# A two-layer streaming encoder on eight cores: score blocks whole, recurrence keys ahead, tap loads on another queue, squares later, last stage in half-size blocks

## The reference, cut to what matters

```python
for i in range(2):                                   # x: 2048 positions x 1024 channels a core
    h = rmsnorm(x, g_mix[i])
    q, f, v, og, glu, ga, gb = split(h @ w_in[i])    # 4 x 512, 1024, 2 x 1024 columns
    # mixer A: per head (4 of 128), S_t = diag(f_t) S_{t-1} + k_t v_t^T ; o_t = S_t^T q_t
    o = rmsnorm(recurrence(silu(q), 1 - f, v, log f)) * silu(og)
    # mixer B: 31 taps over positions, 512 channels
    u = silu(layernorm(causal_dwconv(glu_a * sigmoid(glu_b), conv_w[i])))
    x = x + (sigmoid(ga) * (o @ w_br_a[i]) + sigmoid(gb) * (u @ w_br_b[i])) @ w_out[i]
    up = causal_dwconv(rmsnorm(x, g_ffn[i]) @ w_up[i], 3 taps)
    x = x + (silu(up[..., :2816]) * up[..., 2816:]) @ w_down[i]
    x = x + sigmoid(rmsnorm(x, g_ple[i]) @ w_ple_gate[i]) * (p[i] @ w_ple_proj[i])
return rmsnorm(x, g_final)
```

## Time and profile before

| | |
|---|---|
| median of 3 runs | 2245.28 us (2244.7 to 2246.98) |
| the profiled execution | 2240.89 us |
| its span, slowest core (core 1) | 2239.3 us (all cores 2225.9 to 2239.3) |
| TensorE busy | 2083.4 us |
| VectorE busy | 1403.8 us |
| ScalarE busy | 1077.4 us |
| GpSimd busy | 177.1 us |
| granted TensorE clock, mean over the cores | 0.972 to 0.977 |

### The profile page before, as it was taken

How to read it: one execution, slowest core, us unless ns; L and a number is a source line. 1 busy time by engine, 2 the same in 40 slices (tenths; PEclk the granted TensorE clock), 3 DMA queues, 4 the chain that set the end, 5 groups by cost and what they waited for, 6 DMA issues and landing times.

```text
span 2239.3 us, 29208 instructions; the slowest of 8 cores (2225.9 to 2239.3 us)
## 1 busy us (share of the span) xinstructions
PE 2083.4 (93%) x10176; PEld 983.0 (44%) x10176; DVE 1403.8 (63%) x1861; ACT 1077.4 (48%) x1305; POOL 177.1 (8%) x190
## 2 busy tenths in 40 slices
PE   6988999889999999999898899989999999999985
PEld 1454444544444444444344644445444444444432
DVE  4686357554698349965667645575359852996257
ACT  3645155542677147722455532645247732874143
POOL 2120000000001000010000000000000010001000
PEclk8999999999999999999999999999999999999997
DMA  9946445365544665486446464356354366437434
GB/s 150 169 115 121 63 70 85 114 112 87 76 66 54 88 89 80 53 129 130 67 65 111 109 120 76 44 131 139 55 85 76 51 88 107 76 51 106 61 61 156
DMA packets 220854, 206.35 MB, mean 92 GB/s; under 512 B 19867, under 2 KB 195611, under 8 KB 220710
## 3 DMA queue, kind: packets, MB, share of 16 engines
q0 software_dynamic: 175520, 140.89, 44.2%
q1 hardware_dynamic: 45190, 63.59, 9.2%
HBM read 319.07 MB, written 26.26 MB: 154 GB/s over the span
## 4 chain that ended last, share of the span: by engine, by line
PE 78%; DVE 7%; ACT 7%; issue 4%; DMA 3%; SPq 1%; DVEq 0%; ACTq 0%; POOL 0%; POOLq 0%
PE ps L310 78%; ACT arena L319 5%; DVE arena L323 3%; DVE x_sb L323 1%; ACT L319 1%; DVE arena L327 1%; DMA ws_sb<-w_in 1%; DMA x_sb<-xT 1%; DMA arena<-scr_n 1%; DMA scr_u<-arena 0%; DMA arena<-scr_dg 0%; DVE arena L697 0%; DVE S L323 0%; SPq L774 0%; PE ps L861 0%
## 5 line engine op out<-in xcount | busy, mean ns | idle before, releaser
L310 PE MATMUL ps<-h_sb,ws_sb 128*128 128x512 bf16 x5376 | 1209.7, 383 | 33.4 <-ACT arena L319 16.3
L310 PEld LDWEIGHTS ps<-h_sb,ws_sb 128*128 128x128 bf16 x5376 | 526.3, 99 | 680.1 <-issue 71.4
L310 PE MATMUL ps<-arena,ws_sb 128*128 128x512 bf16 x2816 | 641.7, 383 | 21.5 <-ACT arena L319 10.3
L319 ACT ACTIVATE arena<-ps 128x1024 bf16<-128x1024 f32 (+3 forms) x484 | 400.7, 844 | 375.4 <-PE ps L310 358.4
L327 DVE SCALAR_TENSOR_TENSOR arena<-arena,cv_sb 128x1024 f32<-128x1024 bf16 x352 | 432.1, 1279 | 42.3 <-ACT arena L319 40.8
L310 PEld LDWEIGHTS ps<-arena,ws_sb 128*128 128x128 bf16 x2816 | 276.8, 99 | 362.9 <-issue 40.1
L319 ACT ACTIVATE arena<-x_sb 128x1024 bf16<-128x1024 f32 (+1 forms) x120 | 114.7, 969 | 474.1 <-DVE x_sb L323 364.6
L319 ACT ACTIVATE arena<-ps,cv_sb 128x1024 f32<-128x1024 f32 (+2 forms) x272 | 263.6, 971 | 121.2 <-PE ps L310 93.9
L323 DVE TENSOR_TENSOR arena<-arena 128x1024 bf16<-128x1024 f32 (+3 forms) x252 | 247.3, 1002 | 11.9 <-ACT arena L319 6.6
L319 ACT ACTIVATE arena<-arena 128x512 f32<-128x512 f32 (+3 forms) x256 | 203.2, 811 | 31.6 <-DVE arena L327 13.8
L327 DVE SCALAR_TENSOR_TENSOR arena<-arena,ps 128x1024 f32<-128x1024 f32 x64 | 77.8, 1221 | 188.1 <-PE ps L310 167.5
(11 more groups left out here) (56 smaller groups left out, 698.7 us busy)
## 6 DMA issues: line engine op xcount, KB each, us to landing
ws_sb<-w_up POOLq DMA_DIRECT2D x40, 1024.0 KB, 11.1
ws_sb<-w_in POOLq DMA_DIRECT2D x37, 1024.0 KB, 13.0
ws_sb<-w_down POOLq DMA_DIRECT2D x32, 704.0 KB, 8.5
arena<-scr_dg SPq DMA_DIRECT2D x48, 288.0 KB, 3.1
scr_dg<-arena SPq DMA_DIRECT2D x32, 288.0 KB, 3.5
x_sb<-xT SPq DMA_DIRECT2D x32, 256.0 KB, 8.2
ws_sb<-w_out POOLq DMA_DIRECT2D x8, 1024.0 KB, 11.7
ws_sb<-w_ple_gate POOLq DMA_DIRECT2D x8, 1024.0 KB, 11.6
```

The source lines that it names most:

```text
L310: P.op("pe", lambda e: e.matmul(out_ap, l_ap, r_ap, start=start, stop=stop), reads=[l_t, r_t], writes=[out_t], inc=inc)
L319: P.op("act", lambda e: e.activation(out=out_ap, in_=in_ap, func=func, **kw), reads=[in_t] + list(rd), writes=[out_t])
```

## The change

Eight things are changed together.

1. Scores: for each head one 128x128x128 matmul in place of two of 64 columns. The masks are as before.
2. The tiles for the decays (`elc`, `emc`, `mm_`) are kept track of by half (`t_`), in the same memory.
3. In all mixers but the first, the keys of chunk 0 are taken in `closing`, after the forget gate's matmuls, with another order of banks. The recurrence then starts one fill step later and ends one earlier.
4. `scale` takes its second root from bank 3 (the outputs') instead of bank 0 (the transposes'), both logarithms ahead of both exponentials.
5. `get_dg` loads the taps on Pool's queue.
6. The first branch blocks and the layer norm's steps are emitted in another order.
7. `Acc` has lag 3 in mixer and feed-forward, and in `ple` lag 2 with the square issued one block later. Where the half that is scaled next is at hand, the root is read from the tile and not through DRAM. `scale_steps` takes six steps instead of seven; the tap builds come after it. `ple` evaluates block 0 before `flush`, with tanh in half 0.
8. The last embedding pass is `ple_last`: 16 blocks of 512 positions from single banks, its first tile's root taken after half of them, the last table loaded ahead, and the outputs interleaved.

`rec_steps` is moved up in the file unchanged but for what is shown.

```diff
@@ -250,9 +250,9 @@
...
-        elc = Tl(hsm_sb[:, 0, :], "elc")
-        emc = Tl(hsm_sb[:, 1, :], "emc")
-        mm_ = Tl(hsm_sb[:, 2, :], "m")
+        elc_ = [Tl(hsm_sb[:, 0, :], "elc%d" % i) for i in range(2)]
+        emc_ = [Tl(hsm_sb[:, 1, :], "emc%d" % i) for i in range(2)]
+        mm2_ = [Tl(hsm_sb[:, 2, :], "m%d" % i) for i in range(2)]
...
@@ -531,36 +531,43 @@
...
         class Acc:
-            def __init__(self, hf, keep=False, base=NSCR, lag=1):
-                self.hf, self.keep, self.base, self.lag = hf, keep, base, lag
+            def __init__(self, hf, base=NSCR, rsb=NSCR + 4096, lag=3, late=False, direct=False):
+                self.hf, self.rsb, self.lag, self.late, self.direct = hf, rsb, lag, late, direct
...
             def step(self, oc):
                 if oc >= self.lag:
                     self.sums()
-                self.square(oc)
+                if not self.late:
+                    self.square(oc)
+                elif oc > 0:
+                    self.square(oc - 1)
+                    if oc == 7:
+                        self.square(7)

...
-                rs = AR(self.base + 2048 * (self.lag + 1), 4096, F32, "ars")
+                rs = AR(self.rsb, 4096, F32, "ars")
...
-                if not self.keep:
+                if not self.direct:
...
@@ -570,12 +577,12 @@
...
-        def scale_steps(l, hf, gcol, dst):
-            rs2 = load_rs(hf)
+        def scale_steps(l, hf, gcol, dst, acc=None):
+            rs2 = load_rs(hf) if acc is None else acc[0].rs
             yield
             n = 0
-            for i in range(7):
-                for _ in range(3 if i < 2 else 2):
+            for i in range(6):
+                for _ in range(3 if i < 4 else 2):
...
@@ -616,11 +623,12 @@
...
             for g in range(NG):
+                if g % 2 == 0:
+                    next(side, None)
                 d = ring_[g % 4]
                 build_taps(l, g, d, "dve")
                 P.dma("sp", lambda e, d=d, g=g: e.dma_start(out=dg_t[l][g].ap, in_=d.ap), out_t=dg_t[l][g], in_t=d)
                 if g % 2 == 1:
-                    next(side, None)
                     yield
...
@@ -692,6 +698,7 @@
             def gate_ph2(hd, t_):
...
+                elc, emc, mm_ = elc_[t_], emc_[t_], mm2_[t_]
...
@@ -714,12 +721,96 @@
...
+            p_tr, p_sc, p_kv, p_o, p_ss = bank1[0:5]
...
+            def rec_steps():
...
+                def keys(c):
+                    kt = Ktok[c % 2]
+                    for hd in range(4):
+                        hs = slice(hd * 128, (hd + 1) * 128)
+                        P.op("pe", lambda e, hs=hs: e.transpose(p_trb[:, hs], KT[c].ap[:, hs], ident.ap),
+                             reads=[KT[c], ident], writes=[p_tr], inc=(hd == 3))
+                    act(kt, kt.ap, p_tr, p_trb[:, 0:512], AF.Copy)
+                    for hd in range(4):
+                        hs = slice(hd * 128, (hd + 1) * 128)
+                        mm(p_sc, p_sc.ap[:, hs], KT[c], KT[c].ap[:, hs], QT[c], QT[c].ap[:, hs], True, True, hd == 3)
...
+                def outer(c):
...
+                    tt(b_, h3(b_.ap), b_, h3(b_.ap), elc_[c // 4], elc3[:, :, c:c + 1].to_broadcast([128, 4, 128]), ALU.mult)
+                    if c < 7:
+                        tt(b_, h3(b_.ap), b_, h3(b_.ap), emc_[(c + 1) // 4], emc3[:, :, c + 1:c + 2].to_broadcast([128, 4, 128]), ALU.mult)
...
+                def scale(c):
+                    for p_, q_ in ((p_ss, osq_[0]), (p_o, osq_[1])):
+                        mm(p_, p_.ap, ones, ones.ap, q_, q_.ap, True, True, True)
+                    for p_, o_ in ((p_ss, osd[0]), (p_o, osd[1])):
+                        act(o_, o_.ap, p_, p_.ap, AF.Ln, bias=EPS, scale=1.0 / 128)
+                    for o_ in osd:
+                        act(o_, o_.ap, o_, o_.ap, AF.Exp, scale=-0.5)
...
+                keys(0)
+                yield
...
+            rec = rec_steps()
+
             def closing(u0, u1, names):
                 pt = {}
+                if not early:
+                    set_banks((2, 3, 4, 5, 6, 7, 0, 1), ())
                 for nm in ("f", "q", "v", "og"):
                     for u in (u0, u1):
                         pt[u, nm] = gate_mm(u[0], u[1], nm) if nm in names else None
                     wrel(W[nm])
+                    if nm == "f" and not early:
+                        next(rec)
                 for u in (u0, u1):
                     gate_ev(u[0], u[1], *[pt[u, nm] for nm in ("f", "q", "v", "og")])
                 both(u0, u1)
@@ -766,7 +857,7 @@
                     build_taps(l, g, d, "pool" if g % 2 == 0 else "dve")
                     P.dma("sp", lambda e: e.dma_start(out=dg_t[l][g].ap, in_=d.ap), out_t=dg_t[l][g], in_t=d)
                 else:
-                    P.dma("sp", lambda e: e.dma_start(out=d.ap, in_=dg_t[l][g].ap), out_t=d, in_t=dg_t[l][g])
+                    P.dma("pool", lambda e: e.dma_start(out=d.ap, in_=dg_t[l][g].ap), out_t=d, in_t=dg_t[l][g])
...
@@ -848,93 +939,12 @@
...
-            def rec_steps():
...
-                    for hd in range(4):
-                        b0 = hd * 128
-                        mm(p_sc, p_sc.ap[:, b0 + 64:b0 + 128], KT[c], KT[c].ap[:, b0:b0 + 128], QT[c], QT[c].ap[:, b0 + 64:b0 + 128],
-                           True, True, False)
-                        mm(p_sc, p_sc.ap[0:64, b0:b0 + 64], KT[c], KT[c].ap[:, b0:b0 + 64], QT[c], QT[c].ap[:, b0:b0 + 64],
-                           True, True, hd == 3)
...
-                def scale(c):
-                    for i in range(2):
-                        p_, o_ = (p_ss, p_tr)[i], osd[i]
-                        mm(p_, p_.ap, ones, ones.ap, osq_[i], osq_[i].ap, True, True, True)
-                        act(o_, o_.ap, p_, p_.ap, AF.Ln, bias=EPS, scale=1.0 / 128)
-                        act(o_, o_.ap, o_, o_.ap, AF.Exp, scale=-0.5)
...
-            rec = rec_steps()
-            n_side = 29
+            n_side = 29 if early else 28
             n_main = 28
-            lead = 4
+            lead, tail = (4, 0) if early else (5, 1)
             done = 0
             for i, _ in enumerate(fill_steps()):
-                while done * (n_main - lead) < (i + 1 - lead) * n_side:
+                while done < n_side and done * (n_main - lead - tail) < (i + 1 - lead) * n_side:
                     next(rec, None)
                     done += 1
...
@@ -1012,16 +1022,19 @@
...
             y = [None] * 8
-            for cc in range(4):
-                ln_dve(cc)
+            ln_dve(0)
+            ln_dve(1)
+            branch_a(0, 0)
             ln_act(0)
+            ln_dve(2)
+            ln_dve(3)
             ln_act(1)
-            branch_a(0, 0)
+            branch_a(0, 1)
             ln_act(2)
             ln_act(3)
             to_channels()
-            for oi in range(1, 4):
-                branch_a(0, oi)
+            branch_a(0, 2)
+            branch_a(0, 3)
             for oi in range(4):
                 branch_b(0, oi)
...
-            acc = Acc(hf, base=57344 if l == 0 and hf == 0 else NSCR)
+            acc = Acc(hf, 57344, 61440) if l == 0 and hf == 0 else Acc(hf)
...
-            acc = Acc(hf)
+            acc = Acc(hf, direct=hf == 1)
             pend.append(acc.finish)
+            faccs[hf] = acc
...
@@ -1198,53 +1212,132 @@
...
-            first = pg_mm(0)
-            flush()
...
-            acc = Acc(hf, l == n_layers - 1 and hf == 1, 32768, 2)
-            pend.append(acc.finish)
-            accs.append(acc)
-            for oc in range(8):
+
+            def gated(oc, pg, pp):
                 sg, tp = sg2[oc % 2], tp2[oc % 2]
-                pg, pp = first if oc == 0 else pg_mm(oc)
+                if oc == 0 and hf == 0:
+                    act(sg, sg.ap, pg, pg.ap, AF.Tanh, scale=0.5)
+                    stt(tp, tp.ap, sg, sg.ap, 1.0, pp, pp.ap, ALU.add, ALU.mult)
+                    stt(xs[oc][hf], xs[oc][hf].ap, tp, tp.ap, 0.5, xs[oc][hf], xs[oc][hf].ap, ALU.mult, ALU.add)
+                    return
                 act(sg, sg.ap, pg, pg.ap, AF.Sigmoid)
                 tt(tp, tp.ap, sg, sg.ap, pp, pp.ap, ALU.mult)
                 tt(xs[oc][hf], xs[oc][hf].ap, tp, tp.ap, xs[oc][hf], xs[oc][hf].ap, ALU.add)
+
+            gated(0, *pg_mm(0))
+            flush()
+            acc = Acc(hf, *((32768, 38912) if hf == 0 else (67584, 73728)), lag=2, late=True, direct=hf == 0)
+            pend.append(acc.finish)
+            paccs[hf] = acc
+            for oc in range(8):
+                if oc > 0:
+                    gated(oc, *pg_mm(oc))
                 acc.step(oc)
                 if oc % 4 == 3:
...
+        def ple_last(l, W, h, pbt, pbv):
+            set_banks(range(6), ())
+            wgs = [wtile(W["pg%d" % i]) for i in range(2)]
+            wps = [wtile(W["pp%d" % i]) for i in range(2)]
...
+            ost = [AR(53248 + i * 2048, 2048, F32, "ost%d" % i) for i in range(8)]
+            out_tiles.extend(ost)
```

(78 more changed lines are left out.)

145 lines of the change are left out of this document (62 added, 83 removed).

## The result

The changed kernel takes **2181.92 us** in the median of four runs (2180.59 to 2183.37), the kernel before 2246.13 (2244.70 to 2247.01): ratio 0.9714, 95% interval 0.9699 to 0.9729. It is faster by 64 us, where I forecast 110; the time lies 16 us above the top of my range.

A forecast was written before the change was run, and what follows sets the result against it. The tensor engine, busy 2083.4 of 2239.3 us, was taken as the bound, with waits and slow clock to remove. 14.2 + 15.0 + 6.2 + 13.8 + 54 + 6.5 = 109.7 us gave a median of 2136 us, range 2118 to 2166.

The forecast's parts named there:

- the normalization's end: Mixers' branch stage: new order starts ScalarE's work about 1.8 us earlier, lost again waiting for ucs; priced at nothing.
- Sums' lag: Output and down projections: sums three blocks behind end waits of about 1.85 us, seven times, plus 1.3 in first mixer; 14.2 us.
- Embedding stages: Per-layer embedding passes: shorter edge waits and less slow clock, 15.0 us in layer 0; layer 1 6.2 and 13.8.
- the output-gate weights: Start of the mixer after layer 0's embedding: weights' load awaited; 1.5 us charged for wait and clock (0 to 4.5).
- The last stage: Final embedding half to the kernel's end: 57.1 us instead of 70.9, a gain of 13.8 us.
- The later mixers up to the ucs wait: Three later mixers: interleaved stretch of 71.3 us falls to 52.9, 18.4 less; booked as 18 each, 54 us.
- scores: Mixers: four whole score blocks instead of eight halves save 0.90 us a chunk, 32 chunks, 28.8 us.
- the keys: Later mixers: first keys done in the last gates remove a 2.58 us wait before the first outer product.
- the taps: Later mixers' filter pairs: loading taps on Pool's queue costs 0 to 0.2 us for each of six pairs.
- (a): Rival, mixers: VectorE and ScalarE hold them, removed tensor work turns into waits, half of 60 us lost; 2166 us, chance 0.13.
- (b): Rival, mixers: tap loads from Pool's queue land late, 7.1 us, costing 28 us; 2164 us, chance 0.08.
- (c): Rival, mixers: whole score blocks are worth nothing, 28.8 us less gain; 2165 us, chance 0.05.

The follow-up runs named there:

- the base: The changed kernel with the gate weights gb1 and the branch weights (2 MB) held until ucs has landed; 2150.56 us, ratio 0.9587, in the narrowest of three runs.

## Why the prediction was wrong

**The step that failed** is "ucs is awaited from a DMA chain, the idle time of 4 us ... gathers in one place and the clock may fall", with the verdict that the normalization's end "gives a little ... and takes it back". I priced that at nothing. It gave 3.0 to 3.3 us a mixer ahead of the first branch_b, more than my 1.8, and cost 12.1, 11.9, 12.3 and 10.0 behind it, 46.3 us, where the whole forecast is 45.4 off. I had treated the gather's time as fixed (7.6 us from first issue to last landing in the kernel before) and only asked when it would start; it took 14.2. But the edit moves the end of branch_a(0,3) forward against the gather, and with it the release of ga0's slot: 1 MB that had stood 2.9 us behind the gather now stands in front. I did not count the loads that a moved step releases on Pool's queue. That transfers stretch beside one another was there to be read: 1 MB of w_in took 15.0 us next to the stores, 11.3 in the earlier trace rows.

That the loads cause it is shown, not argued: holding 1 MB halves the step, holding 2 MB leaves 1.0 to 5.1 of it, the order alone brings it into the kernel before wherever the loads meet the gather, and over 160 gathers the length goes with the distance of w_br_a. The DMA: Bandwidth & Descriptors page of the Trainium skill (Queues, rings and completion order) says that each DMA engine takes turns packet by packet between the queues that have work for it; the 4.6 and 11.5 us of a transfer of the same gather, without and with the weights ahead of it, are in line with that, though no run here shows the turns themselves or why it is a factor of 2.5. The two loads act at different places: the branch weights lie beside the gather, gb1 beside the stores, whose last must land before the gather may start. Of the 9.8 us that a wait grew in the mean (0.5 to 10.3), 6.6 are the longer gather and 3.5 the lesser work behind its issue (7.5 to 4.0); of these, 1.1 come back when gb1 is held, and the rest, some 2.4, is the price of the new order by itself. That is the part which my "takes it back" had right: in the base the branch stage gives 8.9 us ahead of the first branch_b, all mixers together, and loses 10.0 behind it.

**Sums' lag** (14.2): 13.0 in the changed kernel, 13.5 by the ratios with the edit undone. Right in the seven later stages, 2.0 us each for my 1.85. In the first mixer, where I had 1.3, it lost 1.0: its sums still wait 2.34 us for ScalarE (1.81 before).

**Embedding stages** (15.0 and 20.0): 17.4 and 18.1. The edge waits are 1.42 us where I had 1.2, and the output-gate weights come late as I feared:

```profile
1112.26 3.61 PE L310 MATMUL ps<-h_sb,ws_sb 128*128 128x512 bf16 x16 [1.42 <-DVE arena L323]
...
1121.21 2.95 PE L310 MATMUL ps<-h_sb,ws_sb 128*128 128x512 bf16 x8 [3.62 <-DMA ws_sb<-w_in]
```

The last stage takes 58.1 us from 2123.72 to the end (57.1 forecast); two sums in it wait for ScalarE's square, 2.05 and 2.52 (the root's table loads stand ahead of it in the code), which I had not seen.

**The later mixers up to the ucs wait** (54): 52.6, near enough, but not by my terms. Up to the branch stage they gave 13.8, 16.0 and 13.5, 43.3 us, where I had 18.4 each; the other 9.2 came from the branch order's first half, which I had booked as taken back. Inside, scores were over-sized (28.8; 13 alone, 18 in the base), the keys were worth 7 to 9, and the taps, which I charged, were worth 11 to 14. The pieces were measured by taking each out alone and don't add up to the whole; still, my errors had opposite signs, and the good sum is luck in good part. The common fault: I priced an edit against the stage as it was, while the others changed what it stood beside. How much of the taps' wait comes from the stage being shorter was not run by itself.

**Rivals.** (a), engines other than TensorE taking over in the mixers, is what ate 9 to 10 us of the scores: right in kind, a third of its size. (b), late taps: the median is 4.4 us, but only 36 of the 48 landed in 3.1 to 5.4; the first four of each later mixer, issued behind bulk loads (at 383.8 us in the second), took 10.6 to 14.6. TensorE waited 0.8 us at most all the same. The hold of Pool's queue by VectorE's casts, which the SBUF — State Buffer page of the Trainium skill (the "DVE blocks DMA" trap) would have allowed, was not tested, and no wait shows one. (c): halves cost TensorE more than wholes in the changed kernel too, eight in 1.19 us at 386.12 with halves against four in 0.39 at 387.23 in the base. The cycles that I took from the Trainium skill's page TensorE: Matmul & The Clock Gate (Back-to-back issue gap) stand there for isolated matmuls, and the page itself says that they count too little at few columns, where each matmul has its own weight load; they were no price for these halves. But a part of (c)'s price came by way of (a). No rival named a DMA that grows longer because another is issued sooner, and that one decided.

## What to carry to other kernels

When an edit moves work forward, list every load whose buffer the moved step frees, and set its issue against each small latency-bound transfer near it: some three to five microseconds of order were worth 10 to 12 of wait. If a bulk load has slack and a gather has none, make the queue of the bulk load wait for the gather; here one wait on Pool, ahead of 2 MB of loads, gave 29 us, and holding 1 MB more than needed took 7 back. Price an edit in the stage as the other edits leave it, and for a batch keep a kernel in which the piece is taken out again.

## What the runs showed of the hardware

- A gather of four transfers of 256 KB from DRAM: one transfer took 4.4 to 4.6 us from its issue to its landing (medians, second mixer), 7.0 with 1 MB of weights issued 0.4 us behind the first issue, and 11.5 with the same 1 MB issued 2.7 us ahead. The whole gather, from first issue to last landing, took 6.5 to 9.6 us in the kernel before and 12.6 to 16.0 in the changed one. The stores before it landed in 2.1 us with no load beside them, in 5.1 and 6.9 beside 2 MB.
- The issuing itself can slow down: the four gathers held SP's queue for 1.91 us in nearly all mixers of the kernel before. In the changed kernel it was 5.4 to 6.2 in the eight cases in which w_br_a had been issued 1.0 us or more ahead, and 1.9 to 5.1 in the other 24.
- Loads of 288 KB on Pool's queue landed in 3.1 to 5.4 us, and in 10.6 to 14.6 where bulk loads had been issued ahead of them.
- Eight matmuls of 64 columns with alternating 128- and 64-wide weights took 1.19 us, four of 128 columns 0.39.
